# Residual stored early, expert sums added to the outputs by accumulating transfers

## The reference, cut to what matters

```
mix = einsum(concat(attn, gm), w_out)
x   = x + gate1 * rms_norm(mix, g_post_mix)        # the residual
h2  = rms_norm(x, g_pre_ffn) * (1 + scale2) + shift2
f   = hier_moe(h2)                                 # two experts per token, weighted
x   = x + gate2 * rms_norm(f, g_post_ffn)          # the output: y_prompt, y_sample
```

## Time and profile before

| | us |
|---|---|
| Runs (3): median, lowest, highest | 692.92, 692.34, 694.98 |
| Profiled execution, its time | 693.16 |
| Its span in the trace | 691.4 |
| VectorE busy | 204.1 (30%) |
| ScalarE busy | 155.7 (23%) |
| GpSimd busy | 123.2 (18%) |
| TensorE busy | 556.6 (81%) |

### The profile page before, as it was taken

How to read it: one execution, slowest core, us unless ns; L and a number is a source line. 1 busy time by engine, 2 the same in 40 slices (tenths; PEclk the granted TensorE clock), 3 DMA queues, 4 the chain that set the end, 5 groups by cost and what they waited for, 6 DMA issues and landing times.

```text
span 691.4 us, 9619 instructions
## 1 busy us (share of the span) xinstructions
PE 556.6 (81%) x3081; PEld 310.5 (45%) x3082; DVE 204.1 (30%) x540; ACT 155.7 (23%) x375; POOL 123.2 (18%) x183
## 2 busy tenths in 40 slices
PE   0569999999889998999973489899999787878700
PEld 0335654444355664455542245454655444444300
DVE  1240321011567774124447311111111011111027
ACT  2520111011145453233331021111111110111132
POOL 1000000003400000100000423333333232331212
PEclk9999999999989999999995599999999999999955
DMA  8999007081599400400054559999999999999073
GB/s 260 404 389 398 25 5 300 1 306 58 137 357 299 62 0 1 153 0 31 30 220 161 209 216 377 410 365 412 409 416 406 396 408 406 410 416 373 29 306 163
DMA packets 56728, 168.11 MB, mean 243 GB/s; under 512 B 11773, under 2 KB 12389, under 8 KB 55793
## 3 DMA queue, kind: packets, MB, share of 16 engines
q1 hardware_dynamic: 48928, 150.71, 57.4%
q0 software_dynamic: 6752, 14.13, 5.7%
q10 hardware_dynamic: 1008, 2.75, 1.0%
HBM read 161.13 MB, written 14.57 MB: 254 GB/s over the span
## 4 chain that ended last, share of the span: by engine, by line
PE 50%; DMA 27%; DVE 9%; SPq 5%; ACT 3%; issue 3%; PEld 1%; PEldq 0%; POOL 0%; ACTq 0%; POOLq 0%; DVEq 0%
DMA ring<-in_w_down_dram 13%; PE ps L595 10%; PE ps L709 10%; PE ps L817 6%; PE ps L496 5%; PE ps L576 5%; DMA w<-in_w_down_dram 4%; DMA ring<-in_w_up_dram 4%; DMA ring<-in_w_in_dram 3%; PE ps L825 3%; PE ps L660 3%; PE ps L577 2%; PE ps L688 2%; SPq L395 2%; PE ps L515 2%
## 5 line engine op out<-in xcount | busy, mean ns | idle before, releaser
L817 PE MATMUL ps<-ring,xt 128*64 128x256 f32 x768 | 95.0, 404 | 18.6 <-DMA ring<-in_w_up_dram 11.9
L817 PEld LDWEIGHTS ps<-ring,xt 128*64 128x64 f32 x768 | 63.2, 145 | 56.8 <-issue 35.6
L595 PE MATMUL ps<-ring,h_t 128*128 128x512 f32 x160 | 69.5, 593 | 0.0
L1259 DVE TENSOR_TENSOR hid<-act_g,ps 128x128 f32<-128x128 f32 x32 | 9.2, 288 | 188.4 <-ACT act_g L1473 188.4
L709 PE MATMUL ps<-ring,mix_t 128*128 128x512 f32 x120 | 53.2, 594 | 0.0
L595 PEld LDWEIGHTS ps<-ring,h_t 128*128 128x128 f32 x160 | 30.1, 190 | 37.6 <-issue 37.6
L817 PE MATMUL ps<-w,xt 128*64 128x256 f32 x352 | 40.4, 382 | 5.9 <-DMA w<-in_w_up_dram 3.6
L825 PE MATMUL ps<-ring,hid_t 128*64 128x512 f32 x176 | 42.6, 605 | 3.0 <-ACT hid_t L1483 2.5
L576 PE MATMUL ps<-ring,h_t 128*128 128x512 f32 x80 | 41.0, 594 | 3.7 <-DVE h_t L970 2.7
L1567 POOL DMA_INDIRECT xg<-h_rows,idx_in x32 | 33.4, 1044 | 28.2 <-POOL idx_in L1564 26.9
L1577 POOL DMA_INDIRECT expert_results<-y_sb,idx_out x32 | 32.8, 1024 | 28.2 <-POOL idx_out L1574 28.2
(11 more groups left out here) (231 smaller groups left out, 690.3 us busy)
## 6 DMA issues: line engine op xcount, KB each, us to landing
ring<-in_w_mod_dram SPq DMA_DIRECT2D x8, 3072.0 KB, 19.6
ring<-in_w_gate_dram SPq DMA_DIRECT2D x22, 1024.0 KB
ring<-in_w_up_dram SPq DMA_DIRECT2D x22, 1024.0 KB
ring<-in_w_down_dram SPq DMA_DIRECT2D x22, 1024.0 KB
w<-in_w_gate_dram SPq DMA_DIRECT2D x10, 1024.0 KB
w<-in_w_up_dram SPq DMA_DIRECT2D x10, 1024.0 KB
w<-in_w_down_dram SPq DMA_DIRECT2D x5, 1024.0 KB
w_6d<-in_w_down_dram SPq DMA_DIRECT2D x5, 1024.0 KB
```

Of the source, the lines that this page charges most:

```text
L595: last = pe.matmul(ps[:, 4 + u % 4, :], h_t[:, k, i * P:(i + 1) * P], w[:, k, :], start=(k == 0), stop=(k == KC - 1))
L817: last = pe.matmul(bank[fh * SLOT:(fh + 1) * SLOT, 0:FE].rearrange("p (a f) -> p a f", a=2), x_t[:, k % 4, (k // 4) * SLOT:(k // 4 + 1) * ...
```

## The change

When `norms` on ScalarE has issued the normalisation of a tile, it also issues a store of the tile's residual from `res` to the rows of the output (`out_rows`), which counts on a new semaphore `res_out`. In the tail, VectorE's multiplication L1302 writes straight to `y_out`, and its addition L1304 and the wait between the two are gone. SyncE's five output stores are gone. In their place GpSimd, behind a wait for all five residual stores, takes the power of tile i and then waits for VectorE's tile i-1 and issues a transfer that adds `y_out` to the rows in memory (`accum_op=ALU.add`). The final wait of SyncE on `f_st` stays.

```diff
--- before.py
+++ after.py
@@ -306,7 +306,7 @@
         back_in = [sem(f"back_in{i}") for i in range(TILES)]
         f_first, f_sum, f_sq, f_ms, f_rs, f_out = (
             sem("fin_" + n) for n in ("first", "sum", "sq", "ms", "rs", "out"))
-        f_st = sem("fin_st")
+        f_st, res_out = sem("fin_st"), sem("res_out")
 
 
         ITEMS = ["m0", "m1", "m2", "qkv", "m3", "gu", "m4", "gv", "m5", "m6", "m7", "wo"]
@@ -361,6 +361,9 @@
                     step(*nth(q, c))
             for e in range(2 + LOOPED * WS, EXPERTS):
                 step(*nth(0, e))
+
+        def out_rows(i):
+            return y_prompt[0] if i == 0 else y_sample[0, (i - 1) * P:i * P, :]
 
         def cond_of(i):
             return 0 if i == 0 else 1
@@ -483,10 +486,6 @@
             sp.wait_ge(e_all, 1)
             for i in range(TILES):
                 sp.dma_start(y_back[:, i], y_dram[i * P:(i + 1) * P]).then_inc(back_in[i], 16)
-            for i in range(TILES):
-                sp.wait_ge(f_out, i + 1)
-                dst = y_prompt[0] if i == 0 else y_sample[0, (i - 1) * P:i * P, :]
-                sp.dma_start(dst, y_out[:, i]).then_inc(f_st, 16)
             sp.wait_ge(f_st, 16 * TILES)
 
 
@@ -1299,9 +1298,8 @@
                     dve.tensor_scalar(stats[:, 6, i:i + 1], stats[:, 5, i:i + 1], 1.0 / D, EPS, ALU.mult, ALU.add).then_inc(f_ms, 1)
                 if i:
                     dve.wait_ge(f_rs, i)
-                    link(dve.scalar_tensor_tensor(y_sum[:, i - 1], y_sum[:, i - 1], stats[:, 7, i - 1:i],
-                                                  gate_bc[:, 1, cond_of(i - 1), :], ALU.mult, ALU.mult))
-                    dve.tensor_tensor(y_out[:, i - 1], res[:, i - 1], y_sum[:, i - 1], ALU.add).then_inc(f_out, 1)
+                    dve.scalar_tensor_tensor(y_out[:, i - 1], y_sum[:, i - 1], stats[:, 7, i - 1:i],
+                                             gate_bc[:, 1, cond_of(i - 1), :], ALU.mult, ALU.mult).then_inc(f_out, 1)
 
 
         @block.scalar
@@ -1427,6 +1425,7 @@
                 if i:
                     act.wait_ge(t2_tr, 2 * i)
                 act.activation(xn2[:], res[:, i], ACT.Copy, scale=stats[:, 7, i:i + 1]).then_inc(xn2_done, 1)
+                act.dma_start(out_rows(i), res[:, i]).then_inc(res_out, 16)
 
             def scale_h2(i):
                 cn = cond_of(i)
@@ -1634,9 +1633,14 @@
             pool.sem_inc(e_all, 1)
             pool.wait_ge(e_in, 16 * (n_extra + 1))
 
-            for i in range(TILES):
-                pool.wait_ge(f_ms, i + 1)
-                rsqrt(stats[:, 7, i:i + 1], stats[:, 6, i:i + 1], 1, f_rs)
+            pool.wait_ge(res_out, 16 * TILES)
+            for i in range(TILES + 1):
+                if i < TILES:
+                    pool.wait_ge(f_ms, i + 1)
+                    rsqrt(stats[:, 7, i:i + 1], stats[:, 6, i:i + 1], 1, f_rs)
+                if i:
+                    pool.wait_ge(f_out, i)
+                    pool.dma_start(out_rows(i - 1), y_out[:, i - 1], accum_op=ALU.add).then_inc(f_st, 16)
 
 
 # ---- launch: one core; inputs and outputs as the reference has them ----

```

## The result

The changed kernel took 697.48 us (median of 20 runs, 694.66 to 700.03), the kernel before 694.62 (20 runs, 691.96 to 696.63) beside it. The ratio is 1.0041, 95% interval 1.0029 to 1.0054: about 2.9 us slower. 1.05 us less was forecast. The profiled execution took 695.96 us against 693.16, and its span went from 691.4 to 694.2.

The account below looks back on a forecast made before the run. The tail was taken as bound by read-back, a ScalarE piece, then gapless VectorE. From 693.16 us, −5.15 (adds and waits) + 4.1 (slower, queued landing) + 0 + 0 gave 692.1 us, range 688.6 to 699.6.

Parts of the forecast that it names:

- What goes: VectorE's tail: five adds (L1304), 6.1 us, removed; after waits on ScalarE and GpSimd the last issue comes 5.15 us earlier.
- The reading of the strip: Profile page's slices: DMA engines near full to the last expert, 0 in one slice, full once more, then fading.
- ScalarE and the early stores: Between normalisation and logits copy: five store issues cost 0, at most 0.33 us; stores cost 0, at most 1.46.
- GpSimd's issues: In the tail, between powers: 0.62 us per adding transfer issued, or 1.5 if VectorE's passes hold it.
- T: Data time per adding transfer of a tile in the tail: 2.5 us chosen, between 1.46 and 2.92.
- The fixed part of an adding transfer: Landing time of GpSimd's transfers besides data: up to 2.3 us, 1.5 ahead of the data and 0.8 behind.
- The step that failed: Kernel's end: last old store lands at 690.5, span ends at 691.4; nothing was forecast to change between them.
- If the last landing is not the end: Sign at the kernel's end: the prediction is wrong if the last transfer's landing does not end it.
- Accumulation is slow: Rival, tail: adding transfers run well under half of 359 GB/s and chain; at 4 us each, 699.6 us; chance 0.27.
- the queueing: Sign in the tail: issue-to-landing time grows from first to last adding transfer if they queue, the last at 6.75 us.
- GpSimd becomes the bound: Rival, tail: GpSimd's issues take 2.1 us each, last issue 2.1 later; 692.7 us; chance 0.06.

Follow-up runs that it names:

- early_stores: Kernel before plus only the five early ScalarE residual stores, SyncE waiting for them ahead of its read-backs: 694.35 against 694.67 us, ratio 0.9997.
- plain_pool: Changed kernel with GpSimd's five transfers overwriting instead of adding: 30.0 us from SyncE's first read-back issue to span end, against 33.45 for the changed kernel.
- late_memset: Kernel before plus a small GpSimd memset behind a wait for the last output store: 36.8 us from first read-back issue to span end, 6.1 longer.
- sp_plain: Kernel before without the residual addition, SyncE storing plainly: 26.3 us from first read-back issue to span end, 4.4 shorter.
- pool_waits: Changed kernel with GpSimd waiting for its five adding transfers, then a small memset: 37.6 us from first read-back issue to span end, 4.1 longer.
- hybrid2: Kernel before with only tiles 0 and 1 by early store and adding transfer: 692.44 us, ratio 0.9956 to the kernel before.
- before_nopow: Kernel before without GpSimd's five powers in the tail: 30.2 us from first read-back issue to span end, against 30.7.
- acc_last: Kernel before with only tile 4 by early store and adding transfer: 35.0 us from first read-back issue to span end, 4.3 longer.
- hybrid3: Kernel before with tiles 0 to 2 by early store and adding transfer: 690.90 against 694.67 us, ratio 0.9942; measured again, 0.9976.

## Why the prediction was wrong

- **What goes**, right. Last pass of VectorE 682.65 forecast, 682.69 measured; the walk through ScalarE's and GpSimd's waits held at each tile to 0.1 us. The reading of the strip was loose: the slice that was called full once more is a 7; no term used it.
- **ScalarE and the early stores**, right: 0 (early_stores). One figure in it was off: tile 4's store, issued at 360.69 among expert loads, landed 7.5 us after issue and not 2.6. It was in by 368.2, still ahead of the load of expert 4, which was issued at 376.75 (376.68 before).
- **GpSimd's issues**, a little low: 0.84 to 1.01 each, not 0.62; a plain one took 0.53 to 0.64 beside the same passes (plain_pool), so it is the adding that costs 0.3, not VectorE. And the last began 0.3 behind its pass: 4.87 us earlier instead of 5.15.
- **T**, the queue's step, nearly right: 2.5 chosen, 2.56 measured between the landings. My reason for going below the upper bound had no row. By the Trainium skill (Collectives: The Full Stack, Part 3, "The bandwidth ceiling") a DMA that adds needs two source reads on one ring, and the collective that adds ran 1.93 times slower than the one that copies. The trace agrees in the main in engine time, 2.8 against 1.2 us: 2.3 times, and between 1.9 and 2.7 for the rounding. That the 2.8 which I had worked out from the page equals this engine time is luck: 1.93 was applied to 1.46, where a plain transfer took 1.2, and the queue's step was neither.
- **The fixed part of an adding transfer**, mis-sized: 2.3, from a plain load. The first transfer, with none before it in the queue, landed 5.5 us after issue, where 2.3 + 2.5 = 4.8 was said. The last one landed 7.4 behind its issue instead of 6.75: 690.4 instead of 689.45, 0.95 us. Some 0.7 of this are the first landing, some 0.2 the four steps behind it. That the last issue came 0.3 late cost nothing, for its transfer had to queue.
- **The step that failed** is the one that was not worked out: "690.5, and the span ends at 691.4". I carried those 0.9 us over as a constant behind the last landing. They were the end of GpSimd's DRAIN, which had begun at 683.0, and which depends on what GpSimd does last. The change gives GpSimd the last work of the kernel, so the 0.9 became 3.8. That is 2.9 of the 3.85 us between forecast (−1.05) and trace (+2.8); the later landing is the other 0.95. "If the last landing is not the end" was one of the prediction's own signs of being wrong, and it is the one that came.

697.48 us lies inside the stated range (688.6 to 699.6), and 0.4% is less than the 0.5% that was called no change. That is the width of the range and not the mechanism: the forecast was to the other side, and the exit was in none of its terms.

None of the rivals had this. "Accumulation is slow" came nearest in sign, but by its sum T had to be 2.72 just to reach the old landing; the step was 2.56, and the landing came out level by the longer fixed part. The time from issue to landing did grow from the first to the last (5.5 to 7.4), as the queueing said. "GpSimd becomes the bound" named the right engine and the wrong part of it.

In sum, by the profiled run: −4.87 (last issue) + 4.8 (landing 7.4 instead of 2.6) + 2.9 (exit) = +2.8. Against the five removed adds of 6.1 us, 1.2 was lost to waits among the engines, 4.8 to a landing that adds and queues, and 2.9 to the exit.

## What to carry to other kernels

Before you move the last work of a kernel to GpSimd, look at the exit rows of all sequencers: with no adding transfer under way its DRAIN ended 6.6 to 7.0 us behind its last instruction, so GpSimd should be done that much before the others. An adding transfer of 512 KB cost over twice the engine time of a plain one, landed 5.3 us or more after issue, and the DRAIN ended 3.4 us or more behind that. Use it for the early tiles, where both are hidden, and finish the last tiles on an engine and a queue that end quickly.

## What was unexpected of the hardware

- GpSimd's DRAIN at exit, from the end of its last instruction: 6.7 us (before), 6.6 (late_memset), 6.7 (sp_plain) and 6.7 (early_stores) with none of its transfers in the tail; 7.0 (plain_pool) and 7.0 (pool_waits) with five; 6.8 (hybrid2) with two adding ones that had landed 6 us before its end. In before_nopow, where it follows the last scatter, it took 6.6 from its own start. VectorE's and ScalarE's ended within 0.1 us of the engine's last instruction. With adding transfers late in the tail it ended 3.6 (after), 3.4 (acc_last) and 3.5 (hybrid3) behind the last landing, which is short of 6.7: it may be that one part runs before the wait for the transfers and one after. What either part does is open; no run here varied it. At the start of the changed program (L1660) GpSimd has a DRAIN too, and that took 0.18 us. So the 6.7 are not the price of every DRAIN; what of the 690 us between makes them (GpSimd's many transfers, for one) was not tested.
- A plain 512 KB store of GpSimd's landed 2.9 us after issue (plain_pool), 0.3 behind SyncE's 2.6; I had taken 3.8, from a load, as the upper bound. An adding one with none ahead of it in the queue took 5.3 (acc_last) to 5.5 (after).
- A wait list can name the wrong engine: the 3.5 us of SyncE at exit stand against TensorE.
